# Squares of a hidden layer turned by one transpose and moved between partition quarters by DMA

## The chip, the cores and the metric

One NeuronCore of a Trainium2 chip runs the program. The metric is the device time of one execution in microseconds (us); lower is better.

## What is computed

A decoder trunk of two layers over 256 tokens of width 2048, in float32. Each layer has a mixer (layer 0: a spatial gating unit beside dilated attention; layer 1: stick-breaking attention) and a squared-ReLU MLP, each between two RMSNorms. The change lies in the MLP alone:

```
def squared_relu_mlp(h, w1, w2):
    return jnp.square(jax.nn.relu(h @ w1)) @ w2        # w1: 2048 x 8192, w2: 8192 x 2048

x = x + rmsnorm(y, norm_post_mix[layer])
h = rmsnorm(x, norm_pre_ffn[layer])
y = squared_relu_mlp(h, ffn_w1[layer], ffn_w2[layer])
x = x + rmsnorm(y, norm_post_ffn[layer])
```

## The kernel before, in words

**Units and ticks.** All weight products are cut into 94 units. A unit multiplies the activations (256 tokens, held transposed: features on the partitions) by a weight block of 2048 x 512 and leaves 2 x 512 sums for each partition in two PSUM banks. It has 8 ticks; a tick takes 256 rows of the block. Each operand is split into a high part and a low part (`w_hi`, `w_lo`; `act_pair`; `hid_hi`, `hid_lo`), and three products are taken (high by high, high by low, low by high), so a tick is 12 matmuls of 128x512 and a unit 96 (all recorded at L1200, in `tick_tokens`).

**Weights.** SyncE (SP) loads each quarter of a unit's block (1 MB, two ticks) into one of four places of `w_raw` (L253). It waits until VectorE has finished with what stood there (`lo_ready`). ScalarE (ACT) makes `w_hi` of a tick (L391, `conv`), and waits for that until TensorE has done the tick four before it, since `w_hi` and `w_lo` are rings of four ticks (`pe_ticks`). VectorE (DVE) makes `w_lo` (L718, `conv`) as soon as ACT's part is there. TensorE waits for `lo_ready` at each tick. So ACT and DVE work up to four ticks ahead of TensorE and cannot get further.

**The order on ACT and DVE.** In `unit(u, post, extras)` slot t (1 to 7) of unit u first does what `extras` names for t, and then the conversion of tick t + 4 of the same unit (t < 4) or tick t - 4 of the next (t >= 4). After the slots comes `post`, the work on the finished unit's sums, and then tick 4 of the next unit. Every engine does its list in order.

**The MLP.** Each layer has four groups of 8 units: four "up" units (j = 0 to 3) give 2048 hidden features in `hid_hi`/`hid_lo`, then four "down" units multiply these by 2048 rows of w2. After an up unit, in `post`:

- ACT reads the sums, scales and takes the ReLU into `qT` (L597, twice), and squares into `kT` (L601). `qT` and `kT` are used here as token-major buffers.
- DVE turns the squares from `kT` back into `qT`, features on the partitions, by `turn` (L825): 16 instructions of 32 partitions x 256 elements. Each turns the 32x32 blocks that go from one partition quarter to one (other) quarter. Six stand in `post`, five in slot 1 and five in slot 2 of the next unit; the last signals `f_turned`.
- In slot 3 of the next unit ACT waits for `f_turned` and copies the high part to `hid_hi` (L606, twice 128x512, each signals `f_hi`); DVE subtracts to `hid_lo` (L1029, twice, signals `f_half` and then `post_done`).

TensorE needs the tiles of up unit 3 in the first down unit: before its tick 6 it waits for `f_half`, before its tick 7 for `post_done` (`squares_ready`, in `ffn` of TensorE). ACT may write the next ReLU into `qT` once `post_done` says that the squares before have been split. In the units after an attention group the buffer `v_sb` holds values; in the MLP it is unused.

GpSimd (POOL) does little: a power of 128x1 or 128x2 (L361) in each norm, and once in each layer a memset of `y_sb` (L375).

Of the kernel before, what the change touches and what calls it, by code (L numbers as in the profile page):

```python
# [104 lines left out]
def trunk_kernel(nc, x_in, pre_mix, post_mix, pre_ffn, post_ffn, ab_w_in, ln_g, ln_b, sgu_w, sgu_b,  # L105
                 ab_w_out, sb_w_in, sb_w_out, ffn_w1, ffn_w2, shapes, out):
    ctx = ExitStack()
    with ctx:  # L108
# [51 lines left out]
        relu_tok, sq_tok, sq_T = q_flat, k_flat, qT  # L160
# [56 lines left out]
        f_relu, f_sq, f_turned, f_hi, f_half = (sem(n) for n in ("f_relu", "f_sq", "f_turned", "f_hi", "f_half"))  # L217
        s_ln = sem("s_ln")
# [23 lines left out]

        block = ctx.enter_context(nc.Block())
# [3 lines left out]
        def _(sp):  # L247
# [7 lines left out]
            def load_unit(u, w, k0, col):  # L255
                for q in range(QUARTERS):
                    load_quarter(u, q, w, k0, col)
# [16 lines left out]
            def load_ffn(u0, layer):  # L274
                w1, w2 = ffn_w1[layer], ffn_w2[layer]
                with sp.Fori(0, FGROUPS - 1) as g:
                    with sp.Fori(0, 4) as j:
                        load_unit(u0 + 8 * g + j, w1, 0, (4 * g + j) * NC)
                    with sp.Fori(0, 4) as j:
                        load_unit(u0 + 8 * g + 4 + j, w2, g * D, j * NC)  # L280
                load_gain(post_ffn, layer, u0 + 1)
                g = FGROUPS - 1
                with sp.Fori(0, 4) as j:
                    load_unit(u0 + 8 * g + j, w1, 0, (4 * g + j) * NC)
                with sp.Fori(0, 4) as j:
                    load_unit(u0 + 8 * g + 4 + j, w2, g * D, j * NC)
# [59 lines left out]
        def _(pool):  # L346
# [24 lines left out]
            for layer in range(LAYERS):  # L371
# [3 lines left out]
                nc.gpsimd.memset(y_sb[:, :, :], 0.0).then_inc(s_y0, 1)  # L375
                for cols in (rs_y0, rs_y1, rs_x) if layer == 0 else (rs_y0, rs_y1):
                    power(cols)
# [3 lines left out]
        def _(act):  # L381
# [205 lines left out]
            def ffn(u0, layer):  # L587
# [15 lines left out]
                def split_hi(g, j):  # L603
                    act.wait_ge(f_turned, f0 + 4 * g + (j + 1))
                    for i in range(0, 4, 2):
                        nc.scalar.activation(hid_hi[:, 4 * j + i:4 * j + i + 2, :], sq_T[:, i:i + 2, :], ACT.Copy  # L606
                                             ).then_inc(f_hi, 1)

                def group_up(g):
                    for j in range(4):  # L610
                        unit(u0 + 8 * g + j, lambda: squares_of(g, j), {3: [lambda: split_hi(g, j - 1)]} if j else None)

                def group_down(g):
                    unit(u0 + 8 * g + 4, nothing, {3: [lambda: split_hi(g, 3)]})
# [18 lines left out]
                for j in range(3):  # L633
# [4 lines left out]
                    unit(u + j, post, {3: [lambda: split_hi(FGROUPS - 1, 3)]} if j == 0 else None)  # L638
# [965 lines left out]
```

## Time and profile before

| | |
|---|---|
| median of 3 runs | 2124.09 us (2123.3 to 2124.84) |
| profiled execution, its own time | 2123.68 us |
| span of the profiled execution | 2121.8 us |
| busy: PE, DVE, ACT, POOL | 2112.4, 1480.9, 1026.6, 16.9 us |
| granted TensorE clock, mean | 0.999 of full speed |
| DMA | 406.81 MB, mean 192 GB/s |

The profile is one execution. PE is TensorE's matmuls, PEld its weight loads, SPq the issuing of DMAs by SyncE. A matmul's record is longer than its share of the time, since matmuls are pipelined; the distance from one start to the next is what counts. The MLP of layer 0 begins at about 335 us, that of layer 1 at about 1417 us, and each takes some 697 us.

### The profile page before, as it was taken

Reading aid. Unit: us, or ns where it says so; the run is one execution under the profiler, and the core shown is the slowest. Engines: PE = TensorE matmul, PEld = TensorE weight load, DVE = VectorE, ACT = ScalarE, POOL = GpSimd, SP = SyncE. Lnnn points to the kernel's source line nnn. Section 1 sums busy time; section 2 is a strip of 40 time slices with the busy share of each in tenths; the row PEclk is TensorE's granted clock in tenths of the full one; section 3 lists DMA queues with packets and bytes.
Section 4 is the critical chain, followed back from the end, with each engine's and each line's share of the span. In section 5 each row is a group of like instructions: output and inputs, shape, how many; then the busy total and the mean of one; then the engine's idle time right before and its main releaser. Section 6 shows DMA issues by size and latency. Waiting matters only on the chain.

```text
span 2121.8 us, 25441 instructions
## 1 busy us (share of the span) xinstructions
PE 2112.4 (100%) x9448; PEld 1749.8 (82%) x9448; DVE 1480.9 (70%) x1924; ACT 1026.6 (48%) x1180; POOL 16.9 (1%) x24
## 2 busy tenths in 40 slices
PE   9999999999999999999999999999999999999998
PEld 7888888888888888888888888888888888888886
DVE  6797867764774775586778778577756855764875
ACT  6444446543543453454545554665434544543543
POOL 0000000000000000000000000000000000000000
PEclk9999999999999999999999999999999999999999
DMA  9655555656655656665555555456556566656553
GB/s 322 208 179 167 192 196 166 207 194 189 196 199 187 186 200 217 182 195 198 178 180 178 179 176 201 160 160 217 196 187 193 180 212 184 198 197 213 184 199 119
DMA packets 204077, 406.81 MB, mean 192 GB/s; under 512 B 6544, under 2 KB 9936, under 8 KB 203472
## 3 DMA queue, kind: packets, MB, share of 16 engines
q1 hardware_dynamic: 203856, 405.50, 58.1%
q8 instruction: 63, 1.03, 0.2%
q14 instruction: 30, 0.25, 0.0%
q10 hardware_dynamic: 128, 0.03, 0.0%
HBM read 403.41 MB, written 2.10 MB: 191 GB/s over the span
## 4 chain that ended last, share of the span: by engine, by line
PE 99%; DVE 0%; issue 0%; DVEq 0%; ACT 0%; POOL 0%; ACTq 0%; POOLq 0%
PE ps L1200 99%; PE ps L1343 1%; DVE x_sb L762 0%; PE ps L1422 0%; DVE act_pair L1107 0%; DVE act_pair L768 0%; DVE y_sb L1077 0%; DVEq L108 0%; DVE w_lo L796 0%; ACT tmp L493 0%; POOL rs_bc L347 0%; PE ps L1536 0%; PE ps L1541 0%; ACTq L108 0%; DVE rst L852 0%
## 5 line engine op out<-in xcount | busy, mean ns | idle before, releaser
L718 DVE TENSOR_TENSOR w_lo<-w_raw,w_hi 128x1024 fp32r<-128x1024 f32 x750 | 910.1, 1224 | 561.8 <-ACT w_hi L391 558.4
L391 ACT ACTIVATE w_hi<-w_raw 128x1024 fp32r<-128x1024 f32 x750 | 788.5, 1060 | 898.6 <-PE ps L1200 895.1
L1200 PE MATMUL ps<-w_hi,act_pair 128*128 128x512 f32 x3456 | 1072.4, 390 | 0.3 <-DVE act_pair L1107 0.2
L1200 PEld LDWEIGHTS ps<-w_hi,act_pair 128*128 128x128 f32 x3456 | 647.3, 188 | 136.4 <-issue 2.2
L1200 PE MATMUL ps<-w_lo,act_pair 128*128 128x512 f32 x1728 | 670.2, 390 | 0.0
L1200 PE MATMUL ps<-w_hi,hid_hi 128*128 128x512 f32 x1280 | 498.7, 390 | 0.0
L1200 PE MATMUL ps<-w_hi,hid_lo 128*128 128x512 f32 x1280 | 498.0, 389 | 0.0
L1200 PE MATMUL ps<-w_lo,hid_hi 128*128 128x512 f32 x1280 | 498.0, 389 | 0.0
L1200 PEld LDWEIGHTS ps<-w_lo,act_pair 128*128 128x128 f32 x1728 | 324.1, 188 | 66.5 <-DVE w_lo L796 0.3
L825 DVE STREAM_TRANSPOSE qT<-kT 32x256 f32<-32x256 f32 x608 | 265.2, 436 | 42.2 <-ACT kT L601 32.8
L1200 PEld LDWEIGHTS ps<-w_hi,hid_lo 128*128 128x128 f32 x1280 | 240.3, 188 | 49.9
L1200 PEld LDWEIGHTS ps<-w_hi,hid_hi 128*128 128x128 f32 x1280 | 240.3, 188 | 49.6
L1200 PEld LDWEIGHTS ps<-w_lo,hid_hi 128*128 128x128 f32 x1280 | 240.3, 188 | 49.5
L606 ACT ACTIVATE hid_hi<-qT 128x512 fp32r<-128x512 f32 x64 | 36.9, 625 | 124.4 <-DVE qT L825 124.4
L825 DVE STREAM_TRANSPOSE kT<-y_sb 32x256 f32<-32x256 f32 x96 | 41.8, 436 | 1.6
L1029 DVE TENSOR_TENSOR hid_lo<-qT,hid_hi 128x512 fp32r<-128x512 f32 x64 | 41.1, 684 | 0.0
L597 ACT ACTIVATE qT<-ps,rst 128x512 f32<-128x512 f32 x64 | 40.1, 676 | 0.0
L601 ACT ACTIVATE kT<-qT 128x1024 f32<-128x1024 f32 x32 | 33.9, 1061 | 1.0
L422 ACT ACTIVATE act_pair<-ps,gpre 128x256 fp32r<-128x256 f32 (+1 forms) x80 | 28.7, 449 | 9.2 <-PE ps L1343 9.2
L768 DVE SCALAR_TENSOR_TENSOR act_pair<-ps,gpre,act_pair 128x256 fp32r<-128x256 f32 (+1 forms) x70 | 28.6, 453 | 3.1 <-ACT act_pair L422 3.0
L493 ACT ACTIVATE tmp<-ps 128x512 f32<-128x512 f32 x20 | 11.8, 591 | 30.7 <-PE ps L1200 22.8
L361 POOL TENSOR_TENSOR rst<-rst,neg_half 128x1 f32<-128x1 f32 (+1 forms) x13 | 7.9, 605 | 2097.7 <-DVE rst L852 2002.3
(102 smaller groups left out, 475.4 us busy)
## 6 DMA issues: line engine op xcount, KB each, us to landing
w_raw<-in_ffn_w_dram SPq DMA_DIRECT2D x256, 1024.0 KB, 5.2
w_raw<-in_sb_w_in_dram SPq DMA_DIRECT2D x48, 1024.0 KB, 5.1
w_raw<-in_ab_w_in_dram SPq DMA_DIRECT2D x36, 1024.0 KB, 5.1
w_raw<-in_ab_w_out_dram SPq DMA_DIRECT2D x16, 1024.0 KB, 5.1
w_raw<-in_sb_w_out_dram SPq DMA_DIRECT2D x16, 1024.0 KB, 5.0
w_raw<-in_ab_w_in_dram SPq DMA_DIRECT2D x6, 512.0 KB, 8.6
x_sb<-in_x_dram SPq DMA_DIRECT2D x8, 256.0 KB, 7.3
gpost<-in_norm_post_mix_dram SPq DMA_DIRECT2D x2, 1024.0 KB, 7.9
```

The source lines that it names most:

```text
L391: nc.scalar.activation(w_hi[:, t % RING, :, :], w_raw[:, t // 2, h:h + 2, :], ACT.Copy).then_inc(hi_ready, 1)
L422: last = nc.scalar.activation(act_hi[:, kt, part], ps[:, x_bank(k, j), i * T + part.start:i * T + part.stop], ACT.Copy, scale=gpre[:, k * ...
L493: nc.scalar.activation(junk[:, 2 * NC:3 * NC], src, ACT.Square, accum_out=ssy[:, b, c:c + 1]).then_inc(s_ssy, 1)
L597: last = nc.scalar.activation(relu_tok[:, b, :], ps[:, 2 * (j % 2) + b, :], ACT.Relu, scale=rst[:, 6 + b:7 + b])
L601: nc.scalar.activation(sq_tok, relu_tok, ACT.Square).then_inc(f_sq, 1)
L606: nc.scalar.activation(hid_hi[:, 4 * j + i:4 * j + i + 2, :], sq_T[:, i:i + 2, :], ACT.Copy).then_inc(f_hi, 1)
L718: nc.vector.tensor_tensor(w_lo[:, t % RING, :, :], w_raw[:, t // 2, h:h + 2, :], w_hi[:, t % RING, :, :].bitcast(F32), ALU.subtract).then_ ...
L768: last = nc.vector.scalar_tensor_tensor(act_lo[:, kt, part], ps[:, x_bank(k, j), i * T + part.start:i * T + part.stop], gpre[:, k * KT + k ...
L825: last = nc.vector.transpose(cols[:, :, :, tp, :], rows[:, :, :, fq, :])
L1029: nc.vector.tensor_tensor(hid_lo[:, tiles, :], sq_T[:, i:i + 2, :], hid_hi[:, tiles, :].bitcast(F32), ALU.subtract).then_inc(done, 1)
L1200: return nc.tensor.matmul(dst, lhsT, rhs, start=start, stop=stop, skip_group_check=True)
L1343: last = nc.tensor.transpose(ps[:, x_bank(k, j), i * T + b * P:i * T + (b + 1) * P], x_sb[:, b, kt * P:(kt + 1) * P], ident)
```

## The change

The squares are turned by one DVE transpose over all 128 partitions, from `kT` into `v_sb`. It turns every 32x32 block within its own partition quarter. What has to reach another quarter is moved afterwards by 16 DMAs from `v_sb` to `qT`, each 32 partitions x 256 elements (32 KB), from every quarter `a` to every quarter `q`. Those of source quarters 0 and 1 are issued by SyncE (8 DMAs), those of 2 and 3 by GpSimd (8 DMAs). Both wait for `f_turned`, which the one transpose now signals, and for `post_done` of the unit before. ACT waits for all 16 before it copies the high part, and this copy and DVE's subtraction stand in slot 5 of the next unit where they stood in slot 3. In `qT` the blocks lie in another order, so the copy and the subtraction read and write with other strides; sizes and counts are the same.

```diff
-        relu_tok, sq_tok, sq_T = q_flat, k_flat, qT
+        relu_tok, sq_tok = q_flat, k_flat
+        sq_cols = v_sb[:, :, :].rearrange("p b n -> p (b n)").rearrange("p (q h b t) -> p q h b t", q=4, h=4, b=TB)
+        sq_moved = qT[:, :, :].rearrange("p h t -> p (h t)").rearrange("p (a x t) -> p a x t", a=4, t=32)
+        def sq_pairs(i):
+            return sq_moved[:, :, TB * i:TB * i + 4, :].rearrange("p a x t -> p x a t")
+        def as_pairs(tiles):
+            return tiles.rearrange("p h (b a t) -> p (h b) a t", b=TB, a=4)
...
+        def move_squares(engine, n, u, quarters, signal):
+            engine.wait_ge(f_turned, n + 1)
+            engine.wait_ge(post_done, u)
+            for a in quarters:
+                for q in range(4):
+                    engine.dma_start(qT[32 * q:32 * q + 32, a, :],
+                                     v_sb[32 * a:32 * a + 32, :, :].rearrange("p b n -> p (b n)")[:, q * T:(q + 1) * T]
+                                     ).then_inc(signal, 16)
...
-            def load_unit(u, w, k0, col):
+            def load_unit(u, w, k0, col, squares=None):
                 for q in range(QUARTERS):
+                    if q == 3 and squares is not None:
+                        move_squares(sp, squares, u - 2, (0, 1), f_moved_sp)
                     load_quarter(u, q, w, k0, col)
...
+                def group(g):
+                    for j in range(4):
+                        load_unit(u0 + 8 * g + j, w1, 0, (4 * g + j) * NC, f0 + 4 * g + (j - 2) if j >= 2 else None)
+                    for j in range(4):
+                        load_unit(u0 + 8 * g + 4 + j, w2, g * D, j * NC, f0 + 4 * g + (j + 2) if j < 2 else None)
...
                 nc.gpsimd.memset(y_sb[:, :, :], 0.0).then_inc(s_y0, 1)
+                for g in range(FGROUPS):
+                    for j in range(4):
+                        move_squares(pool, 16 * layer + 4 * g + j, (U_FFN0, U_FFN1)[layer] + 8 * g + j, (2, 3), f_moved_pool)
...
                 def split_hi(g, j):
-                    act.wait_ge(f_turned, f0 + 4 * g + (j + 1))
+                    for moved in (f_moved_sp, f_moved_pool):
+                        act.wait_ge(moved, 128 * f0 + 512 * g + 128 * (j + 1))
                     for i in range(0, 4, 2):
-                        nc.scalar.activation(hid_hi[:, 4 * j + i:4 * j + i + 2, :], sq_T[:, i:i + 2, :], ACT.Copy
+                        nc.scalar.activation(as_pairs(hid_hi[:, 4 * j + i:4 * j + i + 2, :]), sq_pairs(i), ACT.Copy
                                              ).then_inc(f_hi, 1)
...
-                        unit(u0 + 8 * g + j, lambda: squares_of(g, j), {3: [lambda: split_hi(g, j - 1)]} if j else None)
+                        unit(u0 + 8 * g + j, lambda: squares_of(g, j), {5: [lambda: split_hi(g, j - 1)]} if j else None)
...
-                    unit(u0 + 8 * g + 4, nothing, {3: [lambda: split_hi(g, 3)]})
+                    unit(u0 + 8 * g + 4, nothing, {5: [lambda: split_hi(g, 3)]})
...
                     dve.wait_ge(f_sq, f0 + 4 * g + (j + 1))
-                    turn(sq_T, sq_tok, range(0, 6))
+                    nc.vector.transpose(sq_cols.rearrange("p q h b t -> p b h q t"),
+                                        sq_tok.rearrange("p b (h q f) -> p b h q f", h=4, q=4)).then_inc(f_turned, 1)
...
-                    return {1: [lambda: turn(sq_T, sq_tok, range(6, 11))],
-                            2: [lambda: turn(sq_T, sq_tok, range(11, 16)).then_inc(f_turned, 1)], 3: [split_lo]}
+                    return {5: [split_lo]}
```

Two places show what moves. First ACT, from the end of one up unit to the split of its squares in the next (`qT`, `kT`: ReLU and squares; `hid_hi`: the high part), before:

```order
L597 ACTIVATE qT<-ps,rst 128x512 [waits s_pow,post_done,pe_ticks]
L597 ACTIVATE qT<-ps,rst 128x512
L601 ACTIVATE kT<-qT 128x1024 [waits f_relu]
L391 ACTIVATE w_hi<-w_raw 128x1024 [waits pe_ticks,raw_landed2] x2
L391 ACTIVATE w_hi<-w_raw 128x1024 [waits pe_ticks,raw_landed3]
L606 ACTIVATE hid_hi<-qT 128x512 [waits f_turned]
L606 ACTIVATE hid_hi<-qT 128x512
L391 ACTIVATE w_hi<-w_raw 128x1024 [waits pe_ticks,raw_landed3]
```

and after the change:

```order
L624 ACTIVATE qT<-ps,rst 128x512 [waits s_pow,post_done,pe_ticks]
L624 ACTIVATE qT<-ps,rst 128x512
L628 ACTIVATE kT<-qT 128x1024 [waits f_relu]
L418 ACTIVATE w_hi<-w_raw 128x1024 [waits pe_ticks,raw_landed2] x2
L418 ACTIVATE w_hi<-w_raw 128x1024 [waits pe_ticks,raw_landed3] x2
L418 ACTIVATE w_hi<-w_raw 128x1024 [waits pe_ticks,raw_landed0]
L634 ACTIVATE hid_hi<-qT 128x512 [waits f_moved_pool,f_moved_sp]
L634 ACTIVATE hid_hi<-qT 128x512
L418 ACTIVATE w_hi<-w_raw 128x1024 [waits pe_ticks,raw_landed0]
```

The copy now stands behind two more conversions, the second of them tick 0 of the next unit, and waits for the two counts of DMAs. DVE, from the transposition of one up unit's squares to their low part, before:

```order
L825 STREAM_TRANSPOSE qT<-kT 32x2x4x32 x6
L718 TENSOR_TENSOR w_lo<-w_raw,w_hi 128x1024
L825 STREAM_TRANSPOSE qT<-kT 32x2x4x32 x5
L718 TENSOR_TENSOR w_lo<-w_raw,w_hi 128x1024
L825 STREAM_TRANSPOSE qT<-kT 32x2x4x32 x5
L718 TENSOR_TENSOR w_lo<-w_raw,w_hi 128x1024
L1029 TENSOR_TENSOR hid_lo<-qT,hid_hi 128x512 x2
L718 TENSOR_TENSOR w_lo<-w_raw,w_hi 128x1024 x5
```

and after the change:

```order
L1049 STREAM_TRANSPOSE v_sb<-kT 128x2x4x4x32
L746 TENSOR_TENSOR w_lo<-w_raw,w_hi 128x1024 x5
L1058 TENSOR_TENSOR hid_lo<-qT,hid_hi 128x512 x2
L746 TENSOR_TENSOR w_lo<-w_raw,w_hi 128x1024 x3
```

Five conversions (ticks 4 to 7 and tick 0 of the next unit) stand ahead of the low part where three stood. On SyncE the eight DMAs stand between the third and the fourth quarter of the unit two further on:

```order
L274 DMA w_raw<-in_ffn_w_dram 128x4x512
L260 DMA qT<-v_sb 32x256 [waits post_done,f_turned]
L260 DMA qT<-v_sb 32x256 x7
L274 ISA [waits lo_ready]
L274 DMA w_raw<-in_ffn_w_dram 128x4x512
```

The first of these loads waits for `lo_ready` of tick 5 of the unit between, the last for that of tick 7.

## Rows read from the trace of the kernel before

**Rows 1.** The page: span, busy times (instructions), granted clock in 40 slices.

```profile
span 2121.8 us, 25441 instructions
...
PE 2112.4 (100%) x9448; PEld 1749.8 (82%) x9448; DVE 1480.9 (70%) x1924; ACT 1026.6 (48%) x1180; POOL 16.9 (1%) x24
...
PEclk9999999999999999999999999999999999999999
```

**Rows 2.** The chain that ended last, pieces in order of time: start us, us, what.

```profile
348.90 681.65 PE ps L1200 x3006
...
1430.85 683.02 PE ps L1200 x3012
```

**Rows 3.** Who waited for whom: engine, line, releaser: us in total, times, longest.

```profile
ACT w_hi L391 <- PE ps L1200: 895.1, 562, 4.3
...
ACT hid_hi L606 <- DVE qT L825: 124.4, 32, 3.9
```

**Rows 4.** Timeline of DVE, first down unit: start us, us, what, count [idle before].

```profile
426.06 2.68 DVE L825 STREAM_TRANSPOSE qT<-kT 32x256 f32<-32x256 f32 x6 [1.03 <-ACT kT L601]
...
432.26 1.22 DVE L718 TENSOR_TENSOR w_lo<-w_raw,w_hi 128x1024 fp32r<-128x1024 f32 x1
...
435.79 1.23 DVE L718 TENSOR_TENSOR w_lo<-w_raw,w_hi 128x1024 fp32r<-128x1024 f32 x1
436.94 1.28 DVE L1029 TENSOR_TENSOR hid_lo<-qT,hid_hi 128x512 fp32r<-128x512 f32 x2
438.14 3.49 DVE L718 TENSOR_TENSOR w_lo<-w_raw,w_hi 128x1024 fp32r<-128x1024 f32 x3
```

**Rows 5.** Timeline of PE, starts of ticks: tick 6 of that unit, two later ticks.

```profile
438.78 0.39 PE L1200 MATMUL ps<-w_hi,hid_hi 128*128 128x512 f32 x1
...
501.34 0.39 PE L1200 MATMUL ps<-w_hi,hid_hi 128*128 128x512 f32 x1
...
509.50 0.39 PE L1200 MATMUL ps<-w_hi,act_pair 128*128 128x512 f32 x1
```

**Rows 6.** Timeline of ACT and DVE, one tick of an undisturbed down unit.

```profile
501.54 1.06 ACT L391 ACTIVATE w_hi<-w_raw 128x1024 fp32r<-128x1024 f32 x1 [1.66 <-PE ps L1200]
...
502.63 1.23 DVE L718 TENSOR_TENSOR w_lo<-w_raw,w_hi 128x1024 fp32r<-128x1024 f32 x1 [1.50 <-ACT w_hi L391]
```

**Rows 7.** Timeline of PE and PEld as they start again after a wait.

```profile
330.15 0.19 PEld L1200 LDWEIGHTS ps<-w_hi,hid_hi 128*128 128x128 f32 x1
330.18 0.48 PE L1200 MATMUL ps<-w_hi,hid_hi 128*128 128x512 f32 x1
...
330.50 0.39 PE L1200 MATMUL ps<-w_lo,hid_hi 128*128 128x512 f32 x1
```

**Rows 8.** Costliest groups: what | busy us, mean ns | idle before, releaser.

```profile
L825 DVE STREAM_TRANSPOSE qT<-kT 32x256 f32<-32x256 f32 x608 | 265.2, 436 | 42.2 <-ACT kT L601 32.8
...
L606 ACT ACTIVATE hid_hi<-qT 128x512 fp32r<-128x512 f32 x64 | 36.9, 625 | 124.4 <-DVE qT L825 124.4
...
L1029 DVE TENSOR_TENSOR hid_lo<-qT,hid_hi 128x512 fp32r<-128x512 f32 x64 | 41.1, 684 | 0.0
...
L924 DVE STREAM_TRANSPOSE tmp<-zs 32x384 f32<-32x384 f32 x16 | 9.1, 570 | 0.3
```

**Rows 9.** Lines that issue DMAs: duration ns min/median/max of one issue; and three timelines.

```profile
L253 SPq DMA_DIRECT2D w_raw<-in_ffn_w_dram x256: 372/373/383, 306.8 to 2083.8; - x128
...
10.81 1.90 SPq L300 DMA_DIRECT2D w_raw<-in_ab_w_in_dram  x1
...
433.71 0.37 SPq L253 DMA_DIRECT2D w_raw<-in_ffn_w_dram  x1
```

**Rows 10.** DMA issues of the page: queue, count, KB each, us from issue to landing.

```profile
w_raw<-in_ffn_w_dram SPq DMA_DIRECT2D x256, 1024.0 KB, 5.2
...
out_dram<-x_sb SPq DMA_DIRECT2D x2, 128.0 KB, 2.7
```

**Rows 11.** Timeline of POOL: its instructions on 1024 columns and on one.

```profile
29.96 1.10 POOL L368 TENSOR_SCALAR_AFFINE_SELECT v_sb<-v_sb 128x1024 f32<-128x1024 f32 x1
...
327.03 0.55 POOL L361 TENSOR_TENSOR rst<-rst,neg_half 128x1 f32<-128x1 f32 x1 [265.43 <-DVE rst L852]
```

More of the change, by code:

```diff
@@ L217, in trunk_kernel @@
         f_relu, f_sq, f_turned, f_hi, f_half = (sem(n) for n in ("f_relu", "f_sq", "f_turned", "f_hi", "f_half"))
+        f_moved_sp, f_moved_pool = sem("f_moved_sp"), sem("f_moved_pool")
         s_ln = sem("s_ln")
@@ L275, in load_ffn @@
                 w1, w2 = ffn_w1[layer], ffn_w2[layer]
+                f0 = 16 * layer
+                def group(g):
[3 more added lines that the diff above has]
+                        load_unit(u0 + 8 * g + 4 + j, w2, g * D, j * NC, f0 + 4 * g + (j + 2) if j < 2 else None)
                 with sp.Fori(0, FGROUPS - 1) as g:
[L277 to L280, printed above, removed]
+                    group(g)
                 load_gain(post_ffn, layer, u0 + 1)
[L282 to L286, printed above, removed]
+                group(FGROUPS - 1)
             def load_x(i):
@@ L637, in post @@
                             square_y(total[b], j, b)
-                    unit(u + j, post, {3: [lambda: split_hi(FGROUPS - 1, 3)]} if j == 0 else None)
+                    unit(u + j, post, {5: [lambda: split_hi(FGROUPS - 1, 3)]} if j == 0 else None)
                 for t in range(1, 4):
@@ L1028, in split_lo @@
                             tiles = slice(4 * j + i, 4 * j + i + 2)
-                            nc.vector.tensor_tensor(hid_lo[:, tiles, :], sq_T[:, i:i + 2, :],
-                                                    hid_hi[:, tiles, :].bitcast(F32), ALU.subtract).then_inc(done, 1)
-                    return {1: [lambda: turn(sq_T, sq_tok, range(6, 11))],
-                            2: [lambda: turn(sq_T, sq_tok, range(11, 16)).then_inc(f_turned, 1)], 3: [split_lo]}
+                            nc.vector.tensor_tensor(as_pairs(hid_lo[:, tiles, :]), sq_pairs(i),
+                                                    as_pairs(hid_hi[:, tiles, :].bitcast(F32)), ALU.subtract).then_inc(done, 1)
+                    return {5: [split_lo]}
                 def group_up(g):
```

## Prediction

> **What bounds the kernel now.** I read the page first. TensorE is busy for 2112.4 of 2121.8 us at full clock in all 40 slices, DVE for 70%, ACT for 48% [rows 1]. A busy PE could still hide gaps, so the chain of waits comes next. It is one unbroken piece of matmuls through nearly all of each MLP: 681.65 us for 3006 matmuls, and 683.02 us for 3012, which is 0.2268 us from start to start in both [rows 2]. The timeline gives the same: 26 ticks of 12 matmuls from 438.78 to 509.50 us, 2.72 us for a tick and 21.76 us for a unit [rows 5]. So in the MLP TensorE waits for nothing. The waits of the others say how they hang on it: ACT waits 895.1 us for TensorE to free a slot of the weight ring, and 124.4 us in 32 pieces (once for each up unit) for the transposed squares [rows 3]. That second wait is ACT's own; it reaches TensorE only where a tile or a weight tick comes too late. The change therefore has nothing to win inside the MLPs. DVE's saved time can't shorten them, and whether the new path is late for TensorE decides.
>
> **The clock of one unit.** I call the start of the first down unit of group 0 time 0. It lies six ticks before 438.78, at 422.46 us. Tick 6 is due at 16.32, tick 7 at 19.04.
>
> **What is removed.** Of DVE, 16 x 0.436 = 7.0 us of transposes for each of 32 up units [rows 8]. The one transpose of 1024 columns isn't in the trace. From 256 to 384 columns a transpose grows from 436 to 570 ns [rows 8], 1.05 ns a column, so 1024 columns come to 1.24 us; below, it can't be under the 436 ns of a quarter of its columns, and above it can't well be over the 7.0 us of the sixteen. I take 1.24. DVE's busy time falls by 32 x (6.98 - 1.24) = 184 us, to some 1297 us. On the path this is worth nothing by itself: conversions that DVE makes earlier only wait in the ring, because ACT's are held by TensorE.
>
> **Slot 5 in place of slot 3, which costs time however early the DMAs land.** Before, DVE's two subtractions started at 436.94, or 14.48, and tick 6 was not due before 16.32, with over 1 us to spare [rows 4, 5]. Now they stand behind the conversion of tick 0 of the next unit. ACT can't begin that before TensorE has finished tick 4, at 5 x 2.72 = 13.60. In an undisturbed tick ACT starts 0.20 us and DVE 1.29 us behind the tick's start and DVE needs 1.23 us [rows 5, 6], so DVE ends it at 16.12. The instruction behind a conversion starts 0.08 us before its record ends (436.94 against 435.79 + 1.23) [rows 4]; the first subtraction runs from 16.04 to 16.72 (684 ns [rows 8]), and 0.03 us later, the step from ACT's end to DVE's start in [rows 6], TensorE may load weights. After a wait the first matmul starts 0.03 us behind its weight load and the second 0.32 us later [rows 7], so the second comes at 17.10 where 16.55 (16.32 + 0.23) was due. TensorE is 0.55 us late. The second subtraction is done 0.6 us later, well before tick 7. Only the first down unit asks for fresh tiles this way, once in a group: 8 times, 8 x 0.55 = **4.4 us**.
>
> **The copy on ACT and the subtraction on DVE** keep their sizes; other strides could make them longer. The nearest rows are the same instructions at 625 and 684 ns [rows 8]. I take no change; a quarter more on the subtraction would add 8 x 0.17 = 1.4 us, and a gain I exclude, as the elements stay the same.
>
> **When must the moves have landed?** The first copy must end by 16.01 (0.03 before 16.04) and takes 0.63, so it must start by 15.38. The landing, L, must be no later than about 15.3; each later microsecond costs TensorE one, 8 times. In other units the limit is the weight ring: tick 1 of the next unit is due at 24.48, and behind L come two copies (1.25), ACT's conversion (1.06), DVE's (1.23) and the steps between, 3.6 us, so L up to 20.9 costs nothing there.
>
> **SyncE's eight.** They stand behind the load that waits for tick 5's low part, done at 5.44 + 2.52 = 7.96. SyncE needs 0.23 us to go on (433.71 against 432.26 + 1.22 [rows 4, 9]), so it issues that load at 8.19. An issue takes 0.37 us [rows 9], so the last of the eight starts at about 11.2. Between a 128 KB store's issue and its landing lie 2.7 us [rows 10]: 13.9. They also stand in one queue behind a load of 1 MB that lands 5.2 us after its issue [rows 10], at 13.4; 256 KB at that pace take 1.3 us more: 14.7. Both are in time. The load behind them waits for tick 7's low part in any case (5.44 us after tick 5's), so the 3 us of issuing are hidden.
>
> **GpSimd's eight.** `f_turned` comes at 3.60 (DVE starts at 426.06 [rows 4]) + 1.24 = 4.84; with the same step, POOL starts at 5.07. The last begins 7 issues later and lands 2.7 us after. The trace has no DMA issued by POOL. From below the price of an issue is SyncE's 0.37 us; from above 1.90 us, SyncE's longest with the queues full [rows 9]. POOL's own instructions take 0.55 us for one column and 1.10 us for 1024 [rows 11]. I take 1.10: a DMA of 32 rows of 1 KB is real work for POOL, and it is nearest to the larger instruction. Then L = 5.07 + 7.7 + 2.7 = 15.5, 0.17 us past the limit. The ends: 0.37 gives L = 10.4 and no cost; 1.90 gives 21.1, 5.8 us late, 8 x 5.8 = 46 us.
>
> The page "DMA: Bandwidth & Descriptors" of the Trainium skill speaks against such a change in its section "Rules for kernel authors": many small transfers should be made one, and under 64 KB one pays mostly overhead; these are 32 KB. Its section on the anatomy of one DMA puts the fixed part at about 2.0 us a transfer, so by it the last of POOL's eight would land about 0.6 us earlier than I have it and the whole would cost the 4.4 us of slot 5. No run here shows a DMA from GpSimd yet.
>
> **The sum.** 8 x (0.55 + 0.17) = 5.8 us on the profiled execution's own 2123.68, which is 0.4 us under the median; against the median of 2124.09 it gives **2129.9 us**, 0.27% slower. About 0.2% (4.2 us, or 0.53 us for each of the eight places) is what a measurement of this kernel can tell from no change.
>
> **Rivals.**
> - *GpSimd is slow.* Its issue costs more than 1.2 us, and the copy on ACT waits for it. For it: its instructions are the slowest for their size, and DVE and the load of 1 MB work at the same time. Against it: POOL has nothing else to do. At 1.46 us, L = 18.0 and the cost is 8 x (0.55 + 2.7) = 26 us: 2150. At 1.90 us it is 2175. The page "SBUF — State Buffer" of the Trainium skill has a cause, in "Who interferes with whom": a DVE instruction with two inputs in SBUF holds up a GpSimd instruction that reads SBUF. DVE's conversions are of that kind; if each held one issue for 0.4 us more, that would be the 2150 case. Chance 21%.
> - *The transfers don't overlap.* If each DMA of a queue began only when the last had landed, eight would take 8 x 2.7 = 21.6 us: L = 26.7, 11.4 us late at eight places and 5.8 us late at the other 24 up units: 95 + 139 us, about 2358. Against it: SyncE's loads at the start follow each other in under 2 us and take far longer to land [rows 9, 10]. Chance 5%.
> - *Not slower.* The place is tick 6 of the first down unit, and the point is 0.53 us. If TensorE doesn't pay the 0.12 us of starting again, or DVE's signal goes out before the end of the record (its next instruction starts 0.08 us before that end), a place costs 0.35 to 0.43 us: 2.8 to 3.4 us in all, 2127.2. For it: my margin to this point is 0.02 us if the moves are in time. Against it: POOL has to be fast as well. Chance 18%.
> - *Faster.* DVE's 184 us would have to matter between the MLPs, where TensorE's few microseconds of waiting are. The order there is untouched. By 0.2% or more: 3%.
>
> That leaves 53% for the forecast (0.53 to about 1.4 us for each place). **Range**: 2125.5 to 2150. The lower end takes in most of the third rival, the upper the slow issue up to 1.46 us. Chances: slower 0.79, same 0.18, faster 0.03.
>
> **What the changed profile would show.** DVE busy near 1297 us, with 32 transposes of 128x1024 at 1.24 us; ACT's wait for DVE at the copy of the high part gone, and in its place one for DMAs from `v_sb`, about 0.6 us each; 8 gaps of TensorE of 0.5 to 0.8 us, released by DVE's subtraction into `hid_lo`, each at tick 6 of a first down unit, and none elsewhere in the MLPs; issues of POOL every 1.1 us. Gaps of 2 us and more would mean that POOL is slow; gaps in the up units too, that the transfers don't overlap; no gaps, that my 16.75 against 16.32 is wrong. If ACT stood waiting for SyncE's moves rather than POOL's, the queue behind the 1 MB load would be the step I have wrong.

## The result, and the profile after

| | before | changed |
|---|---|---|
| median of 6 runs, us | 2124.36 (2123.3 to 2124.84) | 2139.69 (2137.4 to 2140.38) |
| profiled execution, us | 2123.68 | 2139.84 |
| its span, us | 2121.8 | 2137.7 |

The changed kernel takes 1.0073 times as long, with a 95% interval of 1.0063 to 1.0083. That is 15.3 us more, where 5.8 were forecast. The page of its profile:

```profile
span 2137.7 us, 25276 instructions
...
PE 2116.1 (99%) x9448; PEld 1749.8 (82%) x9448; DVE 1304.9 (61%) x1444; ACT 1030.0 (48%) x1180; POOL 142.3 (7%) x280
...
L260 POOL DMA_DIRECT2D qT<-v_sb x256 | 125.4, 498 | 1091.0 <-DVE v_sb L1049 1075.7
...
L1049 DVE STREAM_TRANSPOSE v_sb<-kT 128x1024 f32<-128x1024 f32 x32 | 39.9, 1246 | 32.8 <-ACT kT L628 32.8
L634 ACT ACTIVATE hid_hi<-qT 128x512 fp32r<-128x512 f32 x64 | 36.9, 624 | 38.1 <-DMA qT<-v_sb 38.1
L1058 DVE TENSOR_TENSOR hid_lo<-qT,hid_hi 128x512 fp32r<-128x512 f32 x64 | 41.4, 688 | 19.2 <-ACT hid_hi L634 19.0
...
qT<-v_sb POOLq DMA_DIRECT2D x256, 32.0 KB, 2.6
qT<-v_sb SPq DMA_DIRECT2D x256, 32.0 KB, 4.0
```

Against [rows 1], DVE lost 176 us and TensorE, which bounds the kernel, gained 3.7 of busy time. ACT's wait for DVE at the copy of the high part [rows 3] is one for DMAs now, 38.1 us. Where TensorE itself waits stands in the chain. It is no longer one piece of 3006 matmuls [rows 2]; it is cut at the first down unit of every group. The piece of the chain ahead of the third cut:

```profile
782.92 1.24 DVE w_lo L746
...
784.31 0.37 SPq L274
...
784.86 0.52 SPq L260
...
785.44 0.58 SPq L260
...
788.60 0.59 SPq L260
...
789.23 2.62 DMA qT<-v_sb
...
791.87 0.64 ACT hid_hi L634
...
792.53 0.70 DVE hid_lo L1058
...
793.36 3.71 PE ps L1228 x15
```

DVE's low part of tick 5 lets SyncE issue its load; behind it SyncE needs 0.59 us for each move and 0.63 from one to the next; the eighth lands 2.6 us after the start of its issue; copy, subtraction, TensorE. GpSimd isn't in this chain. The timelines at the first down unit show both (GpSimd, SyncE, ACT, DVE, then TensorE):

```profile
427.55 3.91 POOL L260 DMA_DIRECT2D qT<-v_sb  x8 [17.85 <-DVE v_sb L1049]
...
431.22 4.96 SPq L260 DMA_DIRECT2D qT<-v_sb  x8
...
438.76 1.15 ACT L634 ACTIVATE hid_hi<-qT 128x512 fp32r<-128x512 f32 x2 [1.43 <-DMA qT<-v_sb]
...
439.42 1.29 DVE L1058 TENSOR_TENSOR hid_lo<-qT,hid_hi 128x512 fp32r<-128x512 f32 x2 [0.83 <-ACT hid_hi L634]
...
438.50 0.39 PE L1228 MATMUL ps<-w_hi,hid_lo 128*128 128x512 f32 x1
440.17 0.50 PE L1228 MATMUL ps<-w_hi,hid_hi 128*128 128x512 f32 x1 [1.28 <-DVE hid_lo L1058]
440.50 0.40 PE L1228 MATMUL ps<-w_lo,hid_hi 128*128 128x512 f32 x1
```

GpSimd has issued all eight by 431.46, as SyncE begins its own. TensorE's matmul was due at 438.73 and came at 440.17, 1.44 us late. At the eight places it is 1.44, 2.35, 0.85, 0.98, 0.87, 1.09, 0.55 and 0.69 us late (start less the start before, less 0.227), 8.8 us together. Behind each gap the second matmul stands 0.33 us from the first instead of 0.227; with the next few starts that makes about 0.14 us more a place. The second gap has a sequel:

```profile
614.17 0.39 PE L1228 MATMUL ps<-w_hi,hid_lo 128*128 128x512 f32 x1
616.75 0.79 PE L1228 MATMUL ps<-w_hi,hid_hi 128*128 128x512 f32 x1 [2.18 <-DVE hid_lo L1058]
617.33 0.63 PE L1228 MATMUL ps<-w_lo,hid_hi 128*128 128x512 f32 x1
617.76 0.63 PE L1228 MATMUL ps<-w_hi,hid_lo 128*128 128x512 f32 x1
```

The same stretch by windows (busy times with counts, then granted clock, DMA share, GB/s):

```profile
617.50:618.50 1.00, 1.00 (x4) 0.81 (x3) 1.00 (x1) 0.00 (x0) 0.00 (x0) 0.50 0.00 0
...
620.50:621.50 1.00, 1.00 (x6) 0.82 (x5) 0.00 (x0) 0.17 (x1) 0.00 (x0) 1.00 0.86 317
```

TensorE comes back at a granted clock of 0.50, the lower of its two levels (1.2 instead of 2.4 GHz), and the matmuls run 0.43 us apart until 619.9; the granted clock is 0.50 for 3.4 us (616.7 to 620.1). Nine matmuls take 3.69 us (616.75 to 620.44) where 9 x 0.227 = 2.04 were due: 1.65 us, its own restart in it.

The sum for the MLPs: 8.8 + 1.65 + 7 x 0.14 = 11.4 us. The second part of the loss lies at the very end of the program. The drains of GpSimd and SyncE there, before (duration ns min/median/max, first and last start) and after:

```profile
L108 POOLq DRAIN  x1: 647/647/647, 2114.9 to 2114.9; - x1
...
L108 SPq DRAIN  x1: 7/7/7, 2121.6 to 2121.6; - x1
```

```profile
L108 POOLq DRAIN  x1: 11119/11119/11119, 2126.3 to 2126.3; - x1
...
L108 SPq DRAIN  x1: 7/7/7, 2133.1 to 2133.1; - x1
```

SyncE is done with the stores 11.5 us later than before, which is what the MLPs lost. GpSimd's drain used to be over long before that. Now it lasts to 2126.3 + 11.1 = 2137.4 and ends the program, 4.3 us behind SyncE. So 11.5 + 4.4 = 15.9 us of span.

### The profile page after: what moved, and what is told of

It reads as the page before. It is cut to its first block, busy times and chain, and to the rows that moved or that the text cites. A ratio compares the mean times of both kernels' runs of the same rounds, so it can differ in the third digit from the quotient of the medians.

```text
span 2137.7 us, 25276 instructions
## 1 busy us (share of the span) xinstructions
PE 2116.1 (99%) x9448; PEld 1749.8 (82%) x9448; DVE 1304.9 (61%) x1444; ACT 1030.0 (48%) x1180; POOL 142.3 (7%) x280
## 4 chain that ended last, share of the span: by engine, by line
PE 95%; SPq 2%; DMA 1%; DVE 1%; ACT 1%; issue 0%; DVEq 0%; POOL 0%; ACTq 0%; POOLq 0%
PE ps L1228 94%; SPq L260 2%; DMA qT<-v_sb 1%; PE ps L1371 1%; DVE w_lo L746 0%; ACT w_hi L418 0%; DVE hid_lo L1058 0%; ACT hid_hi L634 0%; SPq L274 0%; DVE x_sb L790 0%; PE ps L1450 0%; DVE act_pair L1135 0%; DVE act_pair L796 0%; DVE y_sb L1105 0%; DVEq L108 0%
## 5 line engine op out<-in xcount | busy, mean ns | idle before, releaser
L260 POOL DMA_DIRECT2D qT<-v_sb x256 | 125.4, 498 | 1091.0 <-DVE v_sb L1049 1075.7
L1049 DVE STREAM_TRANSPOSE v_sb<-kT 128x1024 f32<-128x1024 f32 x32 | 39.9, 1246 | 32.8 <-ACT kT L628 32.8
L634 ACT ACTIVATE hid_hi<-qT 128x512 fp32r<-128x512 f32 x64 | 36.9, 624 | 38.1 <-DMA qT<-v_sb 38.1
L853 DVE STREAM_TRANSPOSE qT<-kT 32x256 f32<-32x256 f32 x96 | 41.8, 435 | 1.7
```

The costliest lines, as they stand in the source:

```text
L260: engine.dma_start(qT[32 * q:32 * q + 32, a, :], v_sb[32 * a:32 * a + 32, :, :].rearrange("p b n -> p (b n)")[:, q * T:(q + 1) * T]).then_ ...
L634: nc.scalar.activation(as_pairs(hid_hi[:, 4 * j + i:4 * j + i + 2, :]), sq_pairs(i), ACT.Copy).then_inc(f_hi, 1)
L853: last = nc.vector.transpose(cols[:, :, :, tp, :], rows[:, :, :, fq, :])
L1049: nc.vector.transpose(sq_cols.rearrange("p q h b t -> p b h q t"), sq_tok.rearrange("p b (h q f) -> p b h q f", h=4, q=4)).then_inc(f_turn ...
```

## Experiments

Times are medians, ratios go against the kernel before in the same runs, with their 95% interval. "Places" are the eight first down units.

**Slot 5 without the DMAs.** The kernel before with the copy and the subtraction in slot 5.

```diff
-                        unit(u0 + 8 * g + j, lambda: squares_of(g, j), {3: [lambda: split_hi(g, j - 1)]} if j else None)
+                        unit(u0 + 8 * g + j, lambda: squares_of(g, j), {5: [lambda: split_hi(g, j - 1)]} if j else None)
...
-                    unit(u0 + 8 * g + 4, nothing, {3: [lambda: split_hi(g, 3)]})
+                    unit(u0 + 8 * g + 4, nothing, {5: [lambda: split_hi(g, 3)]})
...
-                    unit(u + j, post, {3: [lambda: split_hi(FGROUPS - 1, 3)]} if j == 0 else None)
+                    unit(u + j, post, {5: [lambda: split_hi(FGROUPS - 1, 3)]} if j == 0 else None)
...
-                            2: [lambda: turn(sq_T, sq_tok, range(11, 16)).then_inc(f_turned, 1)], 3: [split_lo]}
+                            2: [lambda: turn(sq_T, sq_tok, range(11, 16)).then_inc(f_turned, 1)], 5: [split_lo]}
```

> The kernel before (16 transposes, no moves by DMA), with only the copy and the subtraction moved from slot 3 to slot 5. If slot 5 alone costs what the prediction says, TensorE has 8 gaps of about 0.5 us before tick 6 of the first down units and each costs 0.55 to 0.7 us with the slower matmuls behind it: 4.4 to 5.5 us over the kernel before, no longer end of the program (3.3 us from the last update of x to the end, as before). Rival: slot 5 is harmless when nothing is late, 0 us, and all of the changed kernel's loss comes from the moves.

Measured: 2135.53 us, ratio 1.0053 [1.0039, 1.0067], span 2132.4, GpSimd's drain 646 ns. It costs about twice what was expected. DVE at the first down unit, then TensorE:

```profile
433.24 2.25 DVE L825 STREAM_TRANSPOSE qT<-kT 32x256 f32<-32x256 f32 x5
435.51 3.50 DVE L718 TENSOR_TENSOR w_lo<-w_raw,w_hi 128x1024 fp32r<-128x1024 f32 x3
438.93 1.29 DVE L1029 TENSOR_TENSOR hid_lo<-qT,hid_hi 128x512 fp32r<-128x512 f32 x2
...
438.29 0.39 PE L1200 MATMUL ps<-w_hi,hid_lo 128*128 128x512 f32 x1
439.67 0.50 PE L1200 MATMUL ps<-w_hi,hid_hi 128*128 128x512 f32 x1 [0.99 <-DVE hid_lo L1029]
```

With sixteen transposes in DVE's queue three conversions run back to back behind the last of them, so the subtraction starts at 438.93, later than tick 0's conversion alone would have it. The gap is 439.67 - 438.29 - 0.227 = 1.15 us. So slot 5 does open a gap at each place, but its size depends on what DVE still has to do; this run doesn't give the size for the changed kernel, the next one but one does.

**One DMA of GpSimd's.** The kernel before with a single transfer of 128x2 elements at the start.

```diff
+        probe = sb("probe", [P, 2])
...
+        s_probe = sem("s_probe")
...
+            nc.gpsimd.dma_start(probe[:, :], neg_half[:, :]).then_inc(s_probe, 16)
+            pool.wait_ge(s_probe, 16)
```

> The kernel before, with one DMA of 128x2 issued by GpSimd near the start and waited for there; nothing reads it. If it is the mere use of GpSimd's own DMA queue that makes its last drain 11 us long in the changed kernel, the end of the program is about 4.4 us later and the whole costs 4 to 5 us, all of it behind the last update of x. Rival: the drain grows with the number of DMAs (256 there, 1 here): no more than 0.5 us here. A second rival: the drain was long because of work that was still under way, then 0 us too.

Measured: 2124.51 us, ratio 1.0001 [0.9992, 1.001]; the drain takes 740 ns. Using GpSimd's queue at all is not what makes the drain long.

**SyncE's moves one load earlier.** The changed kernel with them ahead of the third quarter's load.

```diff
-                    if q == 3 and squares is not None:
+                    if q == 2 and squares is not None:
```

> The changed kernel, with SyncE's eight moves ahead of the third quarter's load where they stood behind it. If SyncE's row of issues (0.63 us from one to the next, behind that load) makes the landing late, the moves are issued from about 5 us on and land at about 12, ACT waits no more for DMAs, and the 8 gaps shrink to the 0.55 us of slot 5: the MLPs lose 5 us where the changed kernel loses 11.5, in all about 9.5 us over the kernel before (2134) with the 4.4 us at the end. If GpSimd's moves set the landing, nothing changes: 2139.5.

Measured: 2134.24 us, ratio 1.0047 [1.0034, 1.0061], span 2132.7, so 5 us of the 15.9 came back by moving eight issues past one load. In this execution the first MLP also begins 1.1 us later than in the kernel before, ahead of anything that was changed; within the MLPs TensorE loses 5.3 us instead of 11.5. The chain at the third place:

```profile
786.89 1.07 ACT w_hi L418
...
789.12 0.69 DVE hid_lo L1058
...
789.93 7.11 PE ps L1228 x30
```

No DMA stands in it any more. What is left is the conversion of tick 0 ahead of the subtraction, as the prediction had it for slot 5: the first matmul is 0.51 to 0.53 us late (the prediction's 16.78 against 16.32 makes it 0.46), and with the slower restart a place costs 0.65 (0.55 in the prediction), together 5.2. The waits say the same: TensorE waits 2.9 us for DVE's subtraction here and 7.5 in the changed kernel.

**SyncE's moves halved and doubled in number.** The changed kernel; 16 issues of 16 KB in place of 8 of 32 KB.

```diff
-                    engine.dma_start(qT[32 * q:32 * q + 32, a, :],
-                                     v_sb[32 * a:32 * a + 32, :, :].rearrange("p b n -> p (b n)")[:, q * T:(q + 1) * T]
-                                     ).then_inc(signal, 16)
+                    parts = 2 if signal is f_moved_sp else 1
+                    for h in range(parts):
+                        w = T // parts
+                        engine.dma_start(qT[32 * q:32 * q + 32, a, h * w:(h + 1) * w],
+                                         v_sb[32 * a:32 * a + 32, :, :].rearrange("p b n -> p (b n)")[:, q * T + h * w:q * T + (h + 1) * w]
+                                         ).then_inc(signal, 16)
...
-                        act.wait_ge(moved, 128 * f0 + 512 * g + 128 * (j + 1))
+                        m = 2 if moved is f_moved_sp else 1
+                        act.wait_ge(moved, m * 128 * f0 + m * 512 * g + m * 128 * (j + 1))
```

> The changed kernel, with each of SyncE's eight moves cut into two of half the columns (16 issues). If SyncE's issues set the landing and an issue costs the same for half the bytes, the landing is 8 x 0.63 = 5.0 us later in every unit, so the 8 gaps grow by 5 us each: 40 us and more (a lower TensorE clock after gaps of 6 us could add 2 to 4 us to each), 2180 to 2215; the up units stay whole, as the landing at some 21 is just at the limit of the weight ring. If the bytes set the pace, or GpSimd, no change: 2140.

Measured: 2211.28 us, ratio 1.0411 [1.0395, 1.0427]. The time per issue is the same for half the bytes (median 591 ns, sixteen in 10.64 us against eight in 4.96), so SyncE's price goes by the number of transfers. The waits show something the expectation didn't have:

```profile
ACT hid_hi L638 <- DMA qT<-v_sb: 176.4, 32, 7.1
DVE hid_lo L1062 <- ACT hid_hi L638: 157.3, 32, 6.5
PE ps L1232 <- DVE hid_lo L1062: 55.3, 24, 5.6
```

TensorE waits 24 times, not 8: the up units come late too. The last move of a unit lands 1.8 us after its issue at all but one of the places where the chain has it, when GpSimd's eight have long been issued. Behind the gap of 5.8 us at the first place the granted clock was 0.50 in the first 2.6 us and 0.89 on average over the next 4.

**Both shifts undone.** SyncE's moves one load earlier (2134.24 us), and the copy and the subtraction in slot 4 as well; the diff is against that version.

```diff
-                        unit(u0 + 8 * g + j, lambda: squares_of(g, j), {5: [lambda: split_hi(g, j - 1)]} if j else None)
+                        unit(u0 + 8 * g + j, lambda: squares_of(g, j), {4: [lambda: split_hi(g, j - 1)]} if j else None)
...
-                    unit(u0 + 8 * g + 4, nothing, {5: [lambda: split_hi(g, 3)]})
+                    unit(u0 + 8 * g + 4, nothing, {4: [lambda: split_hi(g, 3)]})
...
-                    unit(u + j, post, {5: [lambda: split_hi(FGROUPS - 1, 3)]} if j == 0 else None)
+                    unit(u + j, post, {4: [lambda: split_hi(FGROUPS - 1, 3)]} if j == 0 else None)
...
-                    return {5: [split_lo]}
+                    return {4: [split_lo]}
```

> The changed kernel with SyncE's moves ahead of the third quarter's load, and the copy and the subtraction in slot 4, ahead of the conversion of the next unit's tick 0. If the loss in the MLPs is the late landing and slot 5 and nothing else, both are gone: the landing at about 12 lies before slot 4's turn (12.3), the first subtraction ends at about 14.2 for a tick due at 16.3, TensorE has no gap in either MLP, and what is left over the kernel before is the 4.4 us of GpSimd's last drain: 2128. Rival: some of the loss is in the moves' traffic or in another wait; then gaps remain and it stays above 2130.

Measured: 2128.54 us, ratio 1.0021 [1.0012, 1.0031]. The chain has its one piece for each MLP again, and the drain is as long as before:

```profile
348.62 681.64 PE ps L1228 x3006
...
1430.61 683.02 PE ps L1228 x3012
```

```profile
L108 POOLq DRAIN  x1: 11117/11117/11117, 2114.6 to 2114.6; - x1
```

So the whole loss in the MLPs is order: one slot and one load. The 3.9 us that remain (4.2 of span) are the drain's alone.

**No DMA of GpSimd's.** The same, but GpSimd copies the four blocks that stay in their quarter, and SyncE issues the other twelve moves.

```diff
-                    engine.dma_start(qT[32 * q:32 * q + 32, a, :],
-                                     v_sb[32 * a:32 * a + 32, :, :].rearrange("p b n -> p (b n)")[:, q * T:(q + 1) * T]
-                                     ).then_inc(signal, 16)
+                    if q != a:
+                        engine.dma_start(qT[32 * q:32 * q + 32, a, :],
+                                         v_sb[32 * a:32 * a + 32, :, :].rearrange("p b n -> p (b n)")[:, q * T:(q + 1) * T]
+                                         ).then_inc(signal, 16)
...
-                        move_squares(sp, squares, u - 2, (0, 1), f_moved_sp)
+                        move_squares(sp, squares, u - 2, range(4), f_moved_sp)
...
-                        move_squares(pool, 16 * layer + 4 * g + j, (U_FFN0, U_FFN1)[layer] + 8 * g + j, (2, 3), f_moved_pool)
+                        pool.wait_ge(f_turned, 16 * layer + 4 * g + j + 1)
+                        pool.wait_ge(post_done, (U_FFN0, U_FFN1)[layer] + 8 * g + j)
+                        pool.wait_ge(s_y0, layer + 1)
+                        for a in range(4):
+                            if layer or g or j or a:
+                                pool.wait_ge(f_moved_pool, 64 * layer + 16 * g + 4 * j + a)
+                            nc.gpsimd.tensor_copy(qT[32 * a:32 * a + 32, a, :],
+                                                  v_sb[32 * a:32 * a + 32, :, :].rearrange("p b n -> p (b n)")[:, a * T:(a + 1) * T]
+                                                  ).then_inc(f_moved_pool, 1)
+                pool.wait_ge(f_moved_pool, 64 * layer + 64)
...
-                    for moved in (f_moved_sp, f_moved_pool):
-                        act.wait_ge(moved, 128 * f0 + 512 * g + 128 * (j + 1))
+                    act.wait_ge(f_moved_sp, 192 * f0 + 768 * g + 192 * (j + 1))
+                    act.wait_ge(f_moved_pool, 4 * f0 + 16 * g + 4 * (j + 1))
```

> As sp_early_slot4, but GpSimd issues no DMA: the four blocks that stay in their quarter are copied by GpSimd instructions (32x256, each waits for the one before) and SyncE issues the other twelve moves. If the long drain comes from GpSimd's DMAs, it is back at 0.65 us and the end of the program is 3.3 us behind the last update of x. SyncE's twelve issues take 7.6 us from about 5.1 on, so the landing is at 14.6 to 15; the copy starts there, the first subtraction ends at about 16.1 for a tick due at 16.3: no gap or a very small one, 2124 to 2126, the same as before and not faster, as nothing inside the MLPs can be won. Rival: the landing is later than 15.2, and the 8 gaps are back at some 0.5 us or more each: 2128 and up.

Measured: 2123.53 us, ratio 0.9998 [0.9989, 1.0007]; the drain is back at 646 ns, the first MLP is one piece of 681.70 us. With nothing late the transposition by DMA costs nothing, and DVE's 170 us less gain nothing. The moves landed 1.9 us (median) after their issue here, and 3.2 in the version that it started from. ACT waits 53.8 us for them, more than the 38.1 of the changed kernel, and TensorE loses nothing: ACT's wait counts only where a tile comes late for it.

**GpSimd's moves doubled in number.** The changed kernel with GpSimd's moves halved instead of SyncE's; the diff is against the kernel with SyncE's halved.

```diff
-                    parts = 2 if signal is f_moved_sp else 1
+                    parts = 2 if signal is f_moved_pool else 1
...
-                        m = 2 if moved is f_moved_sp else 1
+                        m = 2 if moved is f_moved_pool else 1
```

> The changed kernel, with each of GpSimd's eight moves cut into two of half the columns (16 issues). GpSimd's issues (0.49 us) then run from 5.1 to 12.9 and land at about 15, still before SyncE's last at 16.0 to 16.7: if SyncE's set the landing, the MLPs stay as they are in the changed kernel (11.5 us over the kernel before). The drain at the end: if it grows with the number of GpSimd's DMAs (10.5 us more for 256, 0.1 for one), 512 make it about 21.6 us long, and the whole 10 us slower than the changed kernel: 2150. If the drain has a fixed long form, 2140.

Measured: 2167.45 us, ratio 1.02 [1.0184, 1.0216]. Sixteen issues took GpSimd 7.8 us (from 427.65 to 435.46), still over before SyncE's last began at 435.69; by the issues alone nothing should have moved, and the expectation of no effect on the MLPs fell. The chain shows why:

```profile
435.06 0.59 SPq L263
...
435.69 4.81 DMA qT<-v_sb
...
440.52 0.64 ACT hid_hi L638
```

SyncE's transfer, unchanged, landed 4.81 us after its issue (median 5.1 of all, GpSimd's own 4.6). Part of the loss is clock again: behind seven of the eight gaps (2.31 to 3.19 us) the granted clock fell to 0.50. Behind the third, of 2.64 us (799.27 to 802.14), it stayed at 1.00, so the length of a gap alone doesn't decide it. The drain stayed at 11.1 us with 512 transfers.

**SyncE's half alone.** The changed kernel without GpSimd's eight, so half of the squares is left as it stood in the buffer.

```diff
-                for g in range(FGROUPS):
-                    for j in range(4):
-                        move_squares(pool, 16 * layer + 4 * g + j, (U_FFN0, U_FFN1)[layer] + 8 * g + j, (2, 3), f_moved_pool)
...
-                    for moved in (f_moved_sp, f_moved_pool):
-                        act.wait_ge(moved, 128 * f0 + 512 * g + 128 * (j + 1))
+                    act.wait_ge(f_moved_sp, 128 * f0 + 512 * g + 128 * (j + 1))
```

> The changed kernel without GpSimd's eight transfers per unit; SyncE's eight stay where they are (half the squares are left as they stood in the buffer, so the output is another one). With GpSimd's there, the last of SyncE's landed 2.6 to 4.8 us after its start in the chain; in the kernel without any of GpSimd's transfers it was 1.9. Theory A (GpSimd's transfers in flight make SyncE's land later): SyncE's still start 0.63 us apart, the last lands about 2 us after its start, the eight gaps of TensorE shrink from 0.55 to 2.35 us to about 0.5, the half clock after the longest goes, the drain goes: 2122 + 8 x 0.65 = about 2129 us. Theory B (SyncE's landing is what it is by itself): only the drain's 4.4 us goes, 2135 us. I expect A.

Measured: 2130.68 us, ratio 1.0032 [1.002, 1.0044], span 2128.3. The waits:

```profile
ACT hid_hi L630 <- DMA qT<-v_sb: 22.1, 32, 1.8
...
PE ps L1224 <- DVE hid_lo L1054: 4.2, 8, 1.2
```

The issues are as before (eight in 4.96 us, median 590 ns each), yet ACT waits 22.1 us instead of 38.1, and TensorE 4.2 instead of 7.5. With the long gap the half clock went too: between 616 and 619 us the clock is 1.00. The eight gaps sum to 5.5 us instead of 8.8, and within the MLPs TensorE loses 6.7 us instead of 11.5. That is nearer to the theory in which GpSimd's transfers delay SyncE's (2129) than to the other (2135). They are not the only cause: the first place still had 3.11 us from issue to landing, behind a load of 1 MB.

**What makes the drain long.** Four kernels. Three are the kernel before with transfers of GpSimd's in the first MLP: 16 and 128 of 128x2 elements, each waited for, and 256 of 128x1, none waited for; the fourth is the version of 2128.54 us, in which GpSimd now waits for its own eight. The diffs are of 128, of 256 and of the fourth, each against what it started from; the one of 16 differs from that of 128 in the number.

```diff
+        probe = sb("probe", [P, 2])
...
+        s_probe = sem("s_probe")
...
+                for i in range(128 if layer == 0 else 0):
+                    nc.gpsimd.dma_start(probe[:, :], neg_half[:, :]).then_inc(s_probe, 16)
+                    pool.wait_ge(s_probe, 16 * i + 16)
```

```diff
+        probe = sb("probe", [P, 256])
...
+        s_probe = sem("s_probe")
...
+                for i in range(256 if layer == 0 else 0):
+                    nc.gpsimd.dma_start(probe[:, i:i + 1], neg_half[:, 0:1]).then_inc(s_probe, 16)
```

```diff
+                        pool.wait_ge(f_moved_pool, 128 * (16 * layer + 4 * g + j + 1))
```

> The kernel before, in which GpSimd issues 16 transfers of 128x2 elements one after the other, early in the first MLP, where it has nothing else to do. One such transfer left GpSimd's drain at the end at 740 ns, 256 and 512 of 32x256 left it at 11.1 us. Theory A (the drain grows with the number of transfers until a ceiling): between 0.8 and 2 us here. Theory B (a threshold that 16 stays under): 0.65 to 0.8 us. Theory C (any more than one is enough): 11.1 us and 2128 us. I expect B, 2124 us; the transfers themselves cost nothing in the MLP.

> As the run with 16, but 128 transfers of 128x2 elements (some 3 us each from issue to landing, so some 400 us of the first MLP's 682). Under theory A (grows with the number until a ceiling) the drain takes 5 to 11 us, and the time is 2124 to 2128; under B with a threshold under 128 it takes 11.1 us and the time is 2128; if the number is not what counts, but that the transfers are 32-partition moves, it stays at 0.65 to 0.8 us and 2124. I expect 11.1 us.

> The kernel before with 256 transfers of 128x1 elements from GpSimd in the first MLP, none of them waited for (some 130 us of GpSimd's time). If the missing wait or the number of 256 makes the long drain, it takes 11.1 us and the time is 2128; if it is the kind of transfer (32 partitions to 32 others) or that the last of them come in the last MLP, it takes 2 us or less and the time is 2124. I expect 11.1 us.

> The version of 2128.54 us (SyncE's moves ahead of the third quarter's load, subtraction back in slot 4), in which GpSimd also waits for its own eight transfers of a unit before it goes on to the next unit; in the runs with 16 and 128 transfers GpSimd waited for each, and its drain at the end was 2.0 and 1.9 us. Theory A (the drain is long because GpSimd never waited for its transfers): the drain falls to 2 us or less and the time to 2124.3. Theory B (it follows the number or kind of transfers, waited for or not): 11.1 us, and 2128.5 us. The MLPs run through in one piece of the chain either way. I expect A, with 60 to 40.

Measured: 2124.64, 2124.72 and 2123.93 us (one run each), and 2128.54 us for the last, ratio 1.0023 [1.0014, 1.0032]. Their drains, one row from each kernel, in that order:

```profile
L108 POOLq DRAIN  x1: 1972/1972/1972, 2115.9 to 2115.9; - x1
```

```profile
L108 POOLq DRAIN  x1: 1891/1891/1891, 2115.9 to 2115.9; - x1
```

```profile
L108 POOLq DRAIN  x1: 3116/3116/3116, 2115.1 to 2115.1; - x1
```

```profile
L108 POOLq DRAIN  x1: 11117/11117/11117, 2114.8 to 2114.8; - x1
```

With 16 the drain is longer than I expected, with 128 and 256 far shorter than the 11.1 us I expected, and waiting didn't shorten the long one. Neither the number of 256 nor a missing wait makes the long drain. What the two groups still differ in is the kind of transfer (32 partitions of 1 KB or 512 bytes to 32 others, against 128 of 4 or 8 bytes) and its place (up to the last MLP, against the first alone). Which of them counts, I didn't settle.

## Why the prediction was right and wrong

The measured 2139.69 us lies in the range of 2125.5 to 2150, and that is luck in good part. The upper part of the range stood there for slow issues on GpSimd, which didn't come. The 9.5 us above the point of 2129.9 come from other things: SyncE's moves, the clock and the end of the program.

- **Right: TensorE bounds, and DVE's time buys nothing.** The transpose took 1.246 us (1.24 forecast), DVE is at 1304.9 us (1297). The version without GpSimd's DMAs, with nothing late, measured the same as before.
- **Right: slot 5.** 0.55 us a place forecast, 0.65 shown where only that is left (5.2 us of the 15.3); half of the difference is the restart, 0.14 where the sum had 0.09. The copy and the subtraction kept their durations (624 and 688 ns).
- **Wrong: "An issue takes 0.37 us, so the last of the eight starts at about 11.2."** That price was a 1 MB load's. One of these moves took 0.59 and 0.63 from start to start. The last started at 13.2 (422.41 is time 0 in the changed kernel, the first started at 431.22: 8.81 + 7 x 0.63), 2 us later than forecast.
- **Wrong: "Both are in time."** It landed 2.3 to 3.9 us after its start where the chain gives it; ACT started at 438.76, which is 16.35, with a limit of 15.38. I had weighed the load of 1 MB ahead of it, but not GpSimd's eight transfers in flight; without those TensorE waited 4.2 us at the eight places instead of 7.5. SyncE, not GpSimd, was the late queue, which is the sign that the prediction named for this step. Issue and landing together are the extra 8.8 - 8 x 0.51 = 4.7 us of gaps: 1.4 stay without GpSimd's transfers (5.5 - 4.1), 3.3 come with them.
- **Wrong, without harm: GpSimd's 1.10 us an issue.** It took 0.50, so its last started at 8.5 and was due to land at 11.2. The term of 0.17 us a place had the wrong engine behind it. DVE's conversions didn't hold its issues either: 0.50 is the median and 0.67 the longest of 256. Nor do the rows show that its instructions are the slowest for their size: 1.10 us for 1024 columns stands beside ACT's 1.06 and DVE's 1.23 [rows 6, 11]. The rival "GpSimd is slow" fell by this, though its sign, a gap of 2 us or more, came at the second place, and "the transfers don't overlap" by the 0.63 us between issues that land 2.6 us later. "Not slower" would have needed gaps of 0.4; they were 0.51 and more.
- **Missing: the half clock** after the gap of 2.35 us, 1.65 us less a restart's 0.14; I had charged every microsecond late as one. Why the clock fell there is open, as another gap of 2.64 us left it at 1.00.
- **Missing: the end of the program.** 4.4 us of GpSimd's drain, in no step of the sum and as large as the slot-5 term. The view of the last instructions shows it at once in the changed kernel; in the trace of before there was nothing to see, as GpSimd issued no DMA.

In short: of the 15.9 us of span, the forecast had 4.4 of slot 5's 5.2, 4.7 came from late moves instead of 1.4, 1.5 from the clock, 4.4 from the drain (sum 15.8).

The page "DMA: Bandwidth & Descriptors" of the Trainium skill, in its section on the anatomy of one DMA, puts the fixed part of a transfer that GpSimd issues at about 2.0 us. The traces show more in the median: 2.6 us in the changed kernel, 4.6 with GpSimd's moves doubled, and 3.9 for the tiny transfers issued one at a time beside the weight loads, where the shortest took 1.6. SyncE's 1.9 us in the kernel without GpSimd's DMAs comes near the figure, which that section gives for GpSimd's alone.

## What to carry to other kernels

Price an issue by a row of the same kind of transfer: eight small moves held SyncE 5 us here, and what is behind and ahead of them in that queue decides, not their bytes. When work is moved off an engine that doesn't bound, ask only what arrives later for the one that does; here one slot and one load of difference were 11.5 us, and with both put right and no DMA left on GpSimd the change was free and worthless. Look at how the program ends as well: an engine that got DMAs may end it.

## What the runs showed of the hardware that I had not expected

- SyncE's issue of a 32-partition move inside SBUF takes 0.59 us, for 32 KB and for 16 KB; its 1 MB load takes 0.37. GpSimd's takes 0.50 for either size.
- Transfers of two queues delay each other's landing: SyncE's took 1.9 us (median, twelve moves) with GpSimd quiet and 3.3 (eight moves) with GpSimd's eight, both ahead of the third quarter's load; behind that load 3.7 with GpSimd quiet, 4.0 with its eight and 5.1 with its sixteen.
- After a gap of 2.35 us the granted clock was 0.50 for 3.4 us; after the gaps of 1.44 us and less it stayed at 1.00. With GpSimd's moves doubled it fell after one of 2.31 us and stayed at 1.00 after one of 2.64.
- GpSimd's drain at the end took 0.65 us without DMAs of its own, 0.74 after one, 1.9 to 3.1 after 16 to 256 tiny ones, 11.1 after 256 or 512 moves of 32 partitions. Why is open.
